# Moving the branch hint of the one-tile expert body from its first instruction to three units ahead of its end

## What is computed

```python
logits = (h @ router_w).astype(jnp.float32) + router_b.astype(jnp.float32)
top_val, top_idx = lax.top_k(logits, TOP_K)
wts = jax.nn.softmax(top_val, axis=-1)
...
y = jnp.zeros_like(h)
for e in range(N_EXPERTS):
    y = y + combine[..., e:e + 1] * _swiglu(h, exp_gate[e], exp_up[e], exp_down[e])
```

## Time and profile before

| | us |
|---|---|
| three runs | 1941.33, 1952.26, 1951.34 |
| their median | 1951.34 |
| the profiled execution | 1945.55 |
| its span, first to last instruction | 1943.2 |

### The profile page before, as it was taken

The page is one execution under the profiler, slowest core; times in us unless marked ns, Lnnn a source line. Parts: engine busy times, 40 slices in busy tenths (PEclk is TensorE's granted clock), DMA queues, the critical chain, the costliest instruction groups (busy, mean ns, idle before and its releaser), DMA issues.

```text
span 1943.2 us, 21372 instructions
## 1 busy us (share of the span) xinstructions
PE 1750.2 (90%) x8068; PEld 1440.1 (74%) x8068; DVE 1299.5 (67%) x1571; ACT 999.9 (51%) x1341; POOL 103.8 (5%) x90
## 2 busy tenths in 40 slices
PE   5899979678999986999689899999999999999994
PEld 4777757557778766898567677888888788888783
DVE  5565455664434347665645555989898889999897
ACT  5753262343322324434334243777777677777681
POOL 1004010040000003000000000000000000000001
PEclk9999989789999997999789899999999999999997
DMA  8552243434433342565135354999999899999892
GB/s 311 179 188 66 65 168 109 141 130 133 129 117 118 120 130 75 171 203 203 59 101 181 123 181 135 345 345 350 350 346 356 295 376 321 369 321 375 290 374 109
DMA packets 198462, 410.93 MB, mean 211 GB/s; under 512 B 12879, under 2 KB 46266, under 8 KB 198330
## 3 DMA queue, kind: packets, MB, share of 16 engines
q1 hardware_dynamic: 195050, 398.20, 59.5%
q0 software_dynamic: 3280, 11.02, 1.8%
HBM read 407.19 MB, written 1.98 MB: 211 GB/s over the span
## 4 chain that ended last, share of the span: by engine, by line
PE 78%; DVE 10%; ACT 4%; DMA 3%; issue 3%; POOL 1%; PEldq 1%; SPq 0%; DVEq 0%; ACTq 0%; PEld 0%; POOLq 0%
PE ps L506 23%; PE ps L508 22%; PE ps L507 22%; DVE w_lo L432 4%; ACT w_hi L426 2%; PE ps L1280 2%; PE ps L1119 2%; PE ps L1253 1%; PE ps L682 1%; ACT hf L1387 1%; PE ps L683 1%; DMA raw<-in_w_mod 1%; DMA raw<-in_exp_gate 1%; DMA raw<-in_exp_up 1%; DVE Y L1781 1%
## 5 line engine op out<-in xcount | busy, mean ns | idle before, releaser
L432 DVE TENSOR_TENSOR w_lo<-raw,w_hi 128x1024 fp32r<-128x1024 f32 (+1 forms) x760 | 904.9, 1233 | 278.1 <-ACT w_hi L426 264.5
L426 ACT CAST w_hi<-raw 128x1024 fp32r<-128x1024 f32 (+1 forms) x760 | 764.6, 1047 | 415.8 <-PE ps L508 351.6
L506 PE MATMUL ps<-w_hi,gT_hi 128*128 128x512 f32 x792 | 315.4, 398 | 1.1 <-DVE Y L2234 1.1
L508 PE MATMUL ps<-w_hi,gT_lo 128*128 128x512 f32 x792 | 310.4, 392 | 0.0
L507 PE MATMUL ps<-w_lo,gT_hi 128*128 128x512 f32 x792 | 309.9, 391 | 0.0
L506 PE MATMUL ps<-w_hi,prodT_hi 128*128 128x512 f32 x528 | 210.0, 398 | 8.8 <-DVE prod_dense L2088 5.2
L508 PE MATMUL ps<-w_hi,prodT_lo 128*128 128x512 f32 x528 | 206.7, 391 | 0.0
L507 PE MATMUL ps<-w_lo,prodT_hi 128*128 128x512 f32 x528 | 206.6, 391 | 0.0
L506 PE MATMUL ps<-w_hi,hT_hi 128*128 128x512 f32 (+1 forms) x408 | 166.6, 408 | 10.4 <-DVE hT_lo L1771 5.2
L508 PEld LDWEIGHTS ps<-w_hi,gT_lo 128*128 128x128 f32 x792 | 149.4, 189 | 32.0
L506 PEld LDWEIGHTS ps<-w_hi,gT_hi 128*128 128x128 f32 x792 | 149.8, 189 | 31.3 <-issue 1.5
(11 more groups left out here) (358 smaller groups left out, 2053.5 us busy)
## 6 DMA issues: line engine op xcount, KB each, us to landing
raw<-in_exp_gate SPq DMA_DIRECT2D x176, 512.0 KB, 5.2
raw<-in_exp_up SPq DMA_DIRECT2D x176, 512.0 KB, 5.2
raw<-in_exp_down SPq DMA_DIRECT2D x176, 512.0 KB, 5.4
raw<-in_w_mod SPq DMA_DIRECT2D x96, 512.0 KB, 4.8
raw<-in_w_in_conv SPq DMA_DIRECT2D x24, 512.0 KB, 6.3
raw<-in_ffn_gate SPq DMA_DIRECT2D x22, 512.0 KB, 4.6
raw<-in_ffn_up SPq DMA_DIRECT2D x22, 512.0 KB, 4.7
raw<-in_ffn_down SPq DMA_DIRECT2D x22, 512.0 KB, 3.7
```

What stands on the lines that cost most here:

```text
L426: nc.scalar.copy(w_hi[:, s, cols], raw[:, n % RAW, cols]).then_inc(sem("w_hi_ready"), 1)
L432: nc.vector.tensor_tensor(w_lo[:, s, cols], raw[:, n % RAW, cols], w_hi[:, s, cols].bitcast(F32), ALU.subtract).then_inc(sem("w_ready"), 1)
L506: nc.tensor.matmul(out, a[0], b[0], start=start, stop=False)
L508: return nc.tensor.matmul(out, a[1], b[0], start=False, stop=stop)
```

## The change

The hint is marked in the callbacks, when the body is the one for one tile and the unit is 30 of 0 to 32. The branch and everything else stay.

```diff
+HINT_AT = FFN_UNITS - 3
...
+            def mark(self, tiles, u):
+                if tiles == 1 and u == HINT_AT:
+                    self.past = self.eng.mark_branch_hint_location()
...
                 with nc.body(f"{name}_one{e}", valid_engines=[self.kind]):
-                    past = eng.mark_branch_hint_location()
                     expert(1, e, tiles0, scat0)
                     self.add(1)
-                    eng.br(f"{name}_next{e}").branch_hint(past)
+                    eng.br(f"{name}_next{e}").branch_hint(self.past)
...
                 def between(u):
+                    route.mark(tiles, u)
...
                 def splits(u):
                     split_in_loop(act, act_split, u, e)
+                    route.mark(tiles, u)
...
                     split_in_loop(dve, dve_split, u, e)
+                    route.mark(tiles, u)
```

## The result

The changed kernel takes 1967.87 us (median of 6 runs, 1963.54 to 1969.73) beside 1945.2 for the kernel before in the same rounds (6 runs, 1941.33 to 1952.26). The ratio is 1.0106, with a 95% interval of 1.0083 to 1.013: slower by some 20.6 us (the two medians lie 22.7 apart); 1971 had been predicted. The profiled execution took 1963.54 us, its span is 1961.7 (before: 1945.55 and 1943.2).

A forecast was written before the change was run, and what follows sets the result against it. The prediction took TensorE to bound the kernel (78% of the chain), any wait there being lost. 20.0 + 3.2 = 23.2 us gave 1968.7 from the profiled execution or 1974.5 from the median; it named 1971, range 1950 to 1986.

The forecast's parts named there:

- The mechanism: One-tile bodies: a pending hint turns the fetch at a page border to the branch's target; late hints leave no border.
- Item 1: VectorE's end branches of experts 1, 2, 4 and 5: four new stalls at a mean of 5.0 us, 20.0 us.
- Item 2: VectorE's last end branch, behind expert 7: a late landing adds 2.7 to 3.8 us to the tail, taken as 3.2.
- T: Theory of the experiments, not the prediction: VectorE's and ScalarE's hints act only at the next page border, TensorE's at once.
- Item 3: ScalarE's end branches: up to six slow landings at 4.1 us, hidden under VectorE's stalls, zero; else some 3 us each.
- Item 4: TensorE's end branches: up to seven slow landings at 5.06 us, 1.1 us standstill each, hidden in its wait for VectorE: zero.
- What would show it: Trace signs: VectorE waiting for `issue` at six boundaries, 20 to 28 us; TensorE's branches 4 to 5 us; pages after branches.
- The late hint acts at once: Rival: at experts' ends the late hint replaces the prefetched page, both existing stalls go, −9.9 us, 1938 us; chance 0.10.
- The rival with the second chance: Rival on the end branches: the hint does nothing, so the time stays the same; chance 0.05.
- The stalls add up: Rival: TensorE's 1.1 us and ScalarE's late casts come on top, some 3 us at six boundaries, 1989 us; chance 0.05.

The follow-up runs named there:

- experiment 5: Changed kernel with the hint of all three engines at unit 15 instead of FFN_UNITS - 3: ratio 1.0066 to the kernel before, 12.9 us slower.
- experiment 6: Kernel before, early hint; VectorE's never-entered three-tile body lengthened so one-tile bodies start within four instructions of a page border: ratio 1.0088, 17.1 us slower.
- experiment 7: Kernel before, early hint; VectorE's never-entered three-tile body lengthened so a page border lies some 31 instructions into each one-tile body: ratio 0.995, 9.7 us faster.
- experiment 8: Late hint on VectorE alone, its never-entered three-tile body lengthened so a page border falls between hint and branch: ratio 0.998 to the kernel before.
- experiment 10: Changed kernel, VectorE's and ScalarE's never-entered three-tile bodies lengthened so a page border follows each one's late hint: ratio 0.9977 to the kernel before, 4.5 us faster.
- experiment 1: Changed kernel with the late hint on VectorE alone, early hint back on ScalarE and TensorE: ratio 1.0111 to the kernel before, 21.6 us slower.
- experiment 2: Changed kernel with the late hint on ScalarE alone, early hint back on VectorE and TensorE: ratio 1.0084 to the kernel before, 16.4 us slower.
- experiment 4: Kernel before with the hint taken out on all engines: ratio 1.0089, 17.3 us slower.
- experiment 9: Changed kernel, only VectorE's never-entered three-tile body lengthened so a page border follows VectorE's late hint: ratio 1.0035 to the kernel before, 6.8 us slower.
- experiment 3: Changed kernel with the late hint on TensorE alone, early hint back on VectorE and ScalarE: ratio 1.0001 to the kernel before.

## Why the prediction was right, step by step

*The mechanism.* Right, as far as the runs show it: the hint is spent at a page border, and 12 instructions ahead of the branch no border was left in any of the six bodies. Experiments 5, 6, 7, 8 and 10 fit it from several sides for VectorE (landings of 0.97 to 3.16 us with a border between hint and branch, 4.27 to 5.61 without), 5 and 10 for ScalarE (0.37 to 0.39 and 3.77 to 3.94). That a hint turns a fetch rather than adds one, as the prediction had it, fits the pages on q14: 12 more in the changed kernel, and 5, 7 and 5 more in experiments 1, 2 and 5, each time as many as there are new late landings. (In experiment 4 it is 16 for 12.) What the prediction said of experts 3 and 6 of the kernel before, a hint "after the choice of the next page", is the case of no border: moving the grid by 48 instructions took both late landings away (5.82 and 4.68 us became 0.97), and 30 more in expert 0 gave one to all six ends (4.27 to 5.38).

*Item 1, four new stalls at 5.0, 20.0 us.* They cost 5.43, 5.02, 5.68 and 6.07, 22.2 in the profiled execution; by the ratio the whole change is worth 20.6. The price was a mean of 5.44 and 4.5. Against experiment 7's kernel the same two stalls are 104.96 − 99.93 = 5.0 and 100.03 − 96.58 = 3.5: the 95.5 us that a stall-free expert 7 was estimated at is 96.6.

*Item 2, the last end branch, 3.2 us.* Right in sign and too large. The rows that answer to the earlier trace rows:

```profile
1928.81 1.23 DVE L2298 TENSOR_TENSOR gT_hi<-ps,gT_hi 128x1024 fp32r<-128x1024 f32 x1 [5.22 <-ACT gT_hi L1692]
1932.11 1.41 DVE L2240 SCALAR_TENSOR_TENSOR Y<-ps,comb,Y 128x512 f32<-128x512 f32 x2 [2.08 <-PE ps L1284]
```

From the start of the one step to the next it is 3.30 us, 2.18 before: +1.1. The late landing takes only 2.96 us there where the other ends have 4.6 to 5.7, and the step before it covers 1.2. Without any hint (experiment 4) it takes 4.86, and from the one step to the next it is 5.17 us: +3.0, the price that was named. So at this end a hint behind which T has no border still saves some 2 us (2.67 to 2.97 us in experiments 1, 5 and 6, too), which neither the prediction nor T has. Why stays open.

*The sum.* 23.2 us stand against 20.6 by the ratio, with an interval of 16.1 to 25.3, and against 22.25 + 0.9 = 23.1 in the profiled execution. That nearness is partly luck: in that execution item 1 came out 2.2 us too small and item 2 2.1 too large.

*Item 3, ScalarE hidden.* Right as a sum, and its other half too: 3 us each where VectorE lands fast (experiment 2: 3.2). What it did not say is that ScalarE alone would have made most of the loss, 16.4 us, so that mending VectorE alone is not enough: experiment 9 does that and keeps 6.8 us.

*Item 4, TensorE late by 5.06 and hidden.* The zero was right, its premise wrong. TensorE's late hint acts even behind the last border: its page comes 3.3 to 5.2 us after the hint at the ends of experts 1 to 6, and ahead of the branch. Where it has no hint the branches do take 3.5 to 5.4 us, and that is hidden where VectorE is late as well (experiment 4). The 1.1 us each that the item has where VectorE lands in time were not put to a test. Why TensorE differs stays open. What the trace shows beside it is the packet: 16 KB on q8 (80 for 1.31 MB), 8 KB on q14 (68 for 0.56 MB).

*What would show it.* The stalls at six boundaries, the 104 to 106 us, ScalarE's gaps and the pages behind the branch came as said. Two signs did not: TensorE's branches stayed fast, and VectorE's wait is not called `issue`, since a second late engine took the name.

*The rivals.* "The late hint acts at once" is true of TensorE behind its last border (a page on q8 3.3 to 5.2 us behind the hint), but for one end of experiments 3, 9 and 10, and is worth nothing there; it is false of the other two. The rival with the second chance, 0.05, is that the hint does nothing; it falls with experiments 4 and 7. The prediction set TensorE's hinted end branches against other branches, around expert 0; experiment 4 has the same branches without the hint, 3.5 to 5.4 us beside 0.29 to 0.41. And in time: without hints 17.3 us slower, with the hint before a border at every end 9.7 us faster. "The stalls add up" falls with experiments 1 and 9.

*The first stretch.* The 4.66 us by which the profiled execution came sooner to its first end branch are not explained; they are within what other executions show.

## What to carry to other kernels

In these runs a prefetch hint on a branch works on ScalarE and VectorE only if a page border of the code (every 128 instructions here, by the estimate above) lies between hint and branch: VectorE then lands in 0.97 to 3.16 us at the ends of experts 1 to 6, else in 4.27 to 5.82. So put it first in the body and then see by the gaps behind the branch in which bodies none follows. A body shorter than a page, VectorE's with 122 instructions from landing to branch, can miss however early its hint is (six ends of six in experiment 6); some instructions in a branch that isn't taken move the grid, with nothing more to execute, and were worth 9.7 us. When two engines are late at one place, the profile names one of them (in the changed kernel ScalarE, though VectorE starts up to 1.8 us later than its cast lets it): look at the gap behind the branch on each engine, and at whether the one starts right at the end of the other's work or later, before you decide that one was the cause.

## What was not expected of the hardware

- The early hint isn't safe either: on one grid it misses at two ends of six, on another at all six (+17.1 us), on a third at none (−9.7).
- TensorE and the other two differ. With a hint some 6 us ahead and no border behind it TensorE's branch takes 0.40 to 0.43 us in the changed kernel (ends of experts 1, 2, 3 and 5); VectorE with one some 8 us ahead lands, at the ends of experts 1 to 6, as late (4.6 to 5.5 in experiment 1) as with none (4.5 to 6.1). But at the end of expert 2 of experiments 3, 9 and 10 its branch took 3.2, 2.8 and 4.3 us, with a page in sequence 0.15 us ahead to 0.55 us behind the hint.
- A border just ahead of the branch gives part of the gain: with some 7 instructions from border to branch VectorE's landing takes 2.1 to 2.9 us (experiment 8) instead of 4.6 to 5.5 (experiment 1, ends of experts 1 to 6). ScalarE has some 6 instructions there in experiment 10, but its page comes 5 us or more ahead of the branch, and it lands in 0.4 us at these ends.
- Unhinted far branches of TensorE, 3.5 to 5.4 us each, added nothing in experiment 4: its 17.3 us over the kernel before are no more than the changed kernel's 20.6. TensorE's waits for VectorE's sum are shorter there, 7.6 us in five, where the changed kernel has 17.0 in six.
